# High weights times high and low activations in one 512-column matmul, in five feed-forward phases of a fused three-layer block

## The chip, the cores and the metric

The kernel runs on one core of a Trainium2 chip, as one launch. The metric is the device time in microseconds (us) of that core; the time given for a kernel is the median of its runs. Times of single instructions are given in nanoseconds (ns) where that reads better.

## The reference: what is computed

The input is a sequence of 256 tokens of width 1024, in float32. It goes through three layers, each a mixer and a feed-forward part, with RMS norms before (and in the first layer also after) each part. The mixers (a gated linear recurrence with attention; a gated recurrence in chunks; attention over blocks) are not touched by the change. The feed-forward parts are:

```
# layer 1
h = rms_norm(x, ffn_norm_pre)
up = causal_dwconv(h @ w_up, conv_f_w, conv_f_b)        # 1024 -> 6144, 3 taps
gate, val = split(up)
x = x + rms_norm((gelu(gate) * val) @ w_down, ffn_norm_post)    # 3072 -> 1024
# layers 2 and 3
g, u = split(rms_norm(x, norm_ffn) @ w13)                # 1024 -> 5632
x = x + (silu(g) * u) @ w2                               # 2816 -> 1024
# at the end
return rms_norm(x, final_norm)
```

Every product must come out at close to float32 precision.

## The kernel before

**Layout.** Activations are held transposed: 128 channels on the partitions, 256 tokens along the free axis, one such unit per 128 channels. A weight matrix is cut into *parts* of 128 x 1024 elements, which hold eight 128 x 128 blocks; 374 parts are streamed from memory in the order in which they are used. An output *tile* is 128 output channels by 256 tokens, 256 columns of float32, the lower half of a PSUM bank. Tiles go round four banks (`BANKS`), parts round four slots (`RING`).

**Three products for one.** Each weight and each activation is split in a high and a low half of the type float32r, and a block's product is the sum of three matmuls into the same 256 PSUM columns: high weights by high activations, high weights by low activations, low weights by high activations (`three`, L1337 to L1339). The product of the low halves is left out. Each matmul is issued with a weight load of its own, so the high weights of a block are loaded twice.

**The engines.** Each takes its own list of instructions in order, and semaphores tie the lists together:

- SyncE (SP) starts the transfer of part c into `raw` once part c - 4 has been split.
- ScalarE (ACT) copies `raw` to `w_hi` (`hi`, L270), four parts ahead of TensorE, as soon as TensorE has finished the part whose slot it takes. In the phases `up1` and `up2` it also applies Silu to the gate tiles (L583), and at the head of each loop of four tiles the activation table is loaded (L578).
- VectorE (DVE) makes `w_lo = raw - w_hi` (`lo`, L658), three parts ahead, and takes tiles out of PSUM: in `up1` and `up2` by multiplying them with the norm's factor `RSTD` (`normed`, L694, out of `pair_tile`), in `down1` and `down2` by adding them to the residual `X` (L1117, in `add_branch`).
- GpSimd (POOL) multiplies gate and value and splits the product into `u_hi` and `u_lo` (`products`, L1283 to L1288), and adds up squares for the norms.
- TensorE (PE) waits for a part to be split (`lo_ready`) and for its bank to have been taken out (`evacuated`), then runs the blocks (`tile`, `after_norm`, `down`). `after_norm` runs the first two tiles of a phase block by block as the norm's input is split, then the matmuls that sum the squares (`stat`, L1368), then the rest of the tiles.

**The phases that the change touches**, in the order of the program, with tiles and blocks per tile:

| phase | tiles | blocks per tile | taken out by |
|---|---|---|---|
| `down` (layer 1) | 8 | 24 | ACT, copy to `M` (L500) |
| `up1` (layer 2) | 44 | 8 | DVE, times `RSTD` (L694) |
| `down1` | 8 | 22 | DVE, added to `X` (L1117) |
| `up2` (layer 3) | 44 | 8 | DVE, times `RSTD` (L694) |
| `down2` | 8 | 22 | DVE, added to `X` (L1117) |

After the last tile of `down`, `down1` and `down2` comes a norm. The phase `up` of layer 1, with its three-tap convolution on DVE and ACT, is not touched.

Of the kernel before, what the change touches and what calls it, by code (L numbers as in the profile page):

```python
# [17 lines left out]
ALU = mybir.AluOpType  # L18
# [55 lines left out]
def build(nc, stream, par_d, x_d, wf_d, table_d, onehot_d, ident_d, mask_d, lmask_d, out_d):  # L74
    scr = nc.dram_tensor("bias_rows", [H_MOBA, P, EXT], F32, kind="Internal")
    row = nc.dram_tensor("bias_row", [H_MOBA, EXT], F32, kind="Internal")
    with ExitStack() as ctx:
# [9 lines left out]
        h_hi = sb("h_hi", [P, C, S], F32R)  # L87
        h_lo = sb("h_lo", [P, C, S], F32R)
        u_hi = sb("u_hi", [P, F1, S], F32R)
        u_lo = sb("u_lo", [P, F1, S], F32R)  # L90
# [18 lines left out]

        X = F[:, 52:60, :]  # L110
# [17 lines left out]
        PRA, PRB = F[:, 70:78, :], F[:, 0:8, :]  # L128

# [18 lines left out]
        def dcol(name, e):  # L148
# [51 lines left out]
            sem(n) for n in ("wf_split", "f_normed", "merge_gate_ready", "result_by_pool", "result_scaled"))  # L200
        square_done, b_done, gelu_done = (sem(n) for n in ("decay_squared", "b_done", "gelu_done"))
# [30 lines left out]
        for t in range(R):  # L232
            SCANS.setdefault(H_FOX + 5 + (2 * t + 1) // 3, []).append(t)
        H_COUNT = {n: 8 * i for i, n in enumerate(["mix", "ffn", "n0", "f0", "n1", "f1"])}
# [26 lines left out]
        def _(act):  # L261
# [13 lines left out]
            def out_of(t):  # L275
                return bank[t % BANKS][:, 0:S]

# [217 lines left out]
            for j in range(F1):  # L495
# [70 lines left out]
            def feed(name, per, norm):  # L566

                for j in range(per * C):
                    multiplied(PART[name] + j)
                    if j < per * C - 1:  # L570
                        hi(0, 0, PART[name] + j + HI_AHEAD)
# [54 lines left out]
            for j in range(3 * C):  # L626
                multiplied(PART["down2"] + j)
                hi(0, 0, PART["down2"] + j + HI_AHEAD)
# [19 lines left out]
        def _(dve):  # L648
# [312 lines left out]
            for j in range(F1):  # L961
                step("down", j)
            add_normed("post2", "ffn_post", C, "n0")
# [144 lines left out]
            def add_branch(name, per, norm):  # L1108

                for j in range(per * C):  # L1110
# [4 lines left out]
                    if j % per == per - 1:  # L1115
                        multiplied(PART[name] + j)
# [4 lines left out]
            def swiglu(name, norm, pairs0):  # L1121
# [701 lines left out]
```

## Time and profile before

| | |
|---|---|
| median of 3 runs | 1211.69 us (1211.56 to 1214.74) |
| the profiled execution | 1212.74 us |
| its span in the trace | 1210.9 us |
| busy in the span: PE, weight loads (PEld), DVE, ACT, POOL | 1185.9, 1170.4, 861.0, 681.3, 376.3 us |
| mean granted TensorE clock | 0.994 of full |
| transferred | 204.5 MB, 169 GB/s over the span |

The busy time of an engine is the union of its instructions' times. Matmuls are pipelined, their ends are modelled, and the next one starts before the one before has ended; so how fast TensorE goes is read from the distances between starts, not from durations. A granted clock of 1.00 is 2.4 GHz, one of 0.50 is 1.2 GHz. The chain is the sequence of work that ended last, followed back from the last instruction. The profiled execution took 1.84 us more than its span, and 1.05 us more than the median.

### The profile page before, as it was taken

How to read it: one execution, taken by the hardware profiler on the slowest of the kernel's cores; microseconds unless marked ns; L12 is line 12 of the kernel's file. 1: busy time of each engine (PE TensorE's matmuls, PEld its weight loads, DVE VectorE, ACT ScalarE, POOL GpSimd, SP SyncE). 2: the span in 40 equal slices, each digit the busy share in tenths (PEclk: the TensorE clock that was granted, in tenths of full speed). 3: DMA queues.
4: the chain of work that ended last, by engine and by line, in shares of the span. 5: the costliest groups of instructions: out<-in, count | busy, mean ns of one | idle time of the engine just before them, and what ended most of it. 6: DMA issues, size and time to landing. Idle time of an engine off the chain costs nothing.

```text
span 1210.9 us, 26036 instructions
## 1 busy us (share of the span) xinstructions
PE 1185.9 (98%) x9714; PEld 1170.4 (97%) x9714; DVE 861.0 (71%) x1233; ACT 681.3 (56%) x1019; POOL 376.3 (31%) x403
## 2 busy tenths in 40 slices
PE   8999999999999999998999989999999999999996
PEld 8999999999999999998999989999999999999996
DVE  7877887967799998448898595556666767555644
ACT  6597655654467777345754555555445546555442
POOL 3345000701445555112000165445220006444321
PEclk9999999999999999999999999999999999999999
DMA  6556433476545566653633246556765436555661
GB/s 221 181 190 212 140 105 107 136 264 197 168 140 175 186 188 186 201 175 100 180 104 116 77 158 193 187 176 193 257 194 189 141 122 189 181 185 176 202 199 68
DMA packets 56567, 204.52 MB, mean 169 GB/s; under 512 B 6640, under 2 KB 6776, under 8 KB 56368
## 3 DMA queue, kind: packets, MB, share of 16 engines
q1 hardware_dynamic: 54288, 197.35, 52.5%
q0 software_dynamic: 1632, 5.11, 1.2%
q8 instruction: 52, 0.85, 0.3%
q10 hardware_dynamic: 576, 1.05, 0.2%
q14 instruction: 19, 0.16, 0.0%
HBM read 202.43 MB, written 2.63 MB: 169 GB/s over the span
## 4 chain that ended last, share of the span: by engine, by line
PE 91%; DVE 6%; ACT 1%; DMA 1%; issue 0%; DVEq 0%; SPq 0%; ACTq 0%
PE bank L1337 26%; PE bank L1338 26%; PE bank L1339 26%; PE bank L1596 2%; PE bank L1430 2%; PE bank L1431 2%; PE bank L1432 2%; DVE w_lo L658 1%; PE bank L1519 1%; DVE h_lo L688 1%; DVE work L813 1%; DVE work L712 1%; PE bank L1508 1%; DVE work L679 1%; PE bank L1527 1%; DMA raw<-in_stream 1%
## 5 line engine op out<-in xcount | busy, mean ns | idle before, releaser
L658 DVE TENSOR_TENSOR w_lo<-raw,w_hi 128x1024 fp32r<-128x1024 f32 x374 | 487.6, 1311 | 148.8 <-ACT w_hi L270 145.6
L1337 PE MATMUL bank<-h_hi,w_hi 128*128 128x256 f32 x1888 | 541.9, 287 | 11.2 <-DVE h_lo L688 6.4
L1338 PE MATMUL bank<-h_lo,w_hi 128*128 128x256 f32 x1888 | 535.5, 284 | 0.0
L1339 PE MATMUL bank<-h_hi,w_lo 128*128 128x256 f32 x1888 | 535.4, 284 | 0.0
L270 ACT ACTIVATE w_hi<-raw 128x1024 fp32r<-128x1024 f32 x374 | 392.0, 1053 | 197.8 <-PE bank L1339 187.1
L1337 PEld LDWEIGHTS bank<-h_hi,w_hi 128*128 128x128 f32 x1888 | 363.3, 192 | 17.7 <-issue 7.6
L1338 PEld LDWEIGHTS bank<-h_lo,w_hi 128*128 128x128 f32 x1888 | 363.4, 192 | 0.3
L1339 PEld LDWEIGHTS bank<-h_hi,w_lo 128*128 128x128 f32 x1888 | 363.5, 193 | 0.0
L1337 PE MATMUL bank<-u_hi,w_hi 128*128 128x256 f32 x868 | 247.4, 285 | 3.1 <-DVE u_lo L1082 2.0
L1339 PE MATMUL bank<-u_hi,w_lo 128*128 128x256 f32 x868 | 246.1, 283 | 0.0
L1338 PE MATMUL bank<-u_lo,w_hi 128*128 128x256 f32 x868 | 246.0, 283 | 0.0
L694 DVE TENSOR_TENSOR work<-bank,work 128x256 f32<-128x256 f32 x218 | 90.3, 420 | 123.1 <-PE bank L1339 119.2
L1337 PEld LDWEIGHTS bank<-u_hi,w_hi 128*128 128x128 f32 x868 | 167.1, 192 | 3.9 <-issue 3.4
L1338 PEld LDWEIGHTS bank<-u_lo,w_hi 128*128 128x128 f32 x868 | 167.1, 192 | 0.0
L1339 PEld LDWEIGHTS bank<-u_hi,w_lo 128*128 128x128 f32 x868 | 167.0, 192 | 0.0
L1283 POOL TENSOR_TENSOR work<-work 128x256 f32<-128x256 f32 x68 | 82.6, 1215 | 178.0 <-ACT work L583 119.3
L1288 POOL TENSOR_TENSOR u_lo<-work,u_hi 128x256 f32 x68 | 70.1, 1030 | 11.4 <-POOL u_hi L1286 11.4
L1266 POOL TENSOR_TENSOR work<-work 128x256 f32<-128x256 f32 x39 | 29.8, 765 | 134.7 <-DVE work L1117 79.6
L583 ACT ACTIVATE work<-work 128x256 f32<-128x256 f32 x44 | 18.3, 416 | 74.0 <-PE bank L1339 74.0
L1430 PE MATMUL bank<-w_hi,h_hi 128*128 128x256 f32 x192 | 54.9, 286 | 0.0
L1432 PE MATMUL bank<-w_lo,h_hi 128*128 128x256 f32 x192 | 54.3, 283 | 0.0
L1431 PE MATMUL bank<-w_hi,h_lo 128*128 128x256 f32 x192 | 54.3, 283 | 0.0
(229 smaller groups left out, 1211.2 us busy)
## 6 DMA issues: line engine op xcount, KB each, us to landing
raw<-in_stream SPq DMA_DIRECT2D x374, 512.0 KB, 3.7
bias_rows<-bias_row POOLq DMA_DIRECT2D x1, 1536.0 KB, 15.1
work<-in_x_t SPq DMA_DIRECT2D x2, 512.0 KB, 6.3
work<-in_x_t POOLq DMA_DIRECT2D x1, 1024.0 KB, 6.0
work<-bias_rows POOLq DMA_DIRECT2D x1, 1024.0 KB, 12.6
out<-work ACTq DMA_DIRECT2D x4, 256.0 KB, 2.5
work<-in_lmask POOLq DMA_DIRECT2D x1, 512.0 KB, 7.2
work<-bias_rows POOLq DMA_DIRECT2D x1, 512.0 KB, 8.1
```

The costliest lines, as they stand in the source:

```text
L270: A(w_hi[:, slot, :], raw[:, slot, :], ACT.Copy).then_inc(hi_ready, 1)
L658: v.tensor_tensor(w_lo[:, slot, :], raw[:, slot, :], w_hi[:, slot, :].bitcast(F32), ALU.subtract).then_inc(lo_ready, 1)
L694: v.tensor_tensor(dst, out_of(t), RSTD, ALU.mult).then_inc(evacuated, 1)
L1266: chain.wait(g.tensor_tensor(SQT, src[:, c, :], src[:, c, :], ALU.mult))
L1283: g.tensor_tensor(PB[:, pair, :], GB[:, pair, :], YB[:, 2 * pair + 1, :], ALU.mult).then_inc(pair_free, 1)
L1288: g.tensor_tensor(dst_l, PB[:, pair:pair + 1, :], dst_h.bitcast(F32), ALU.subtract).then_inc(ul_ready, 1)
L1337: mm(out, w_hi[:, slot, s], r_hi, start=start, stop=False)
L1338: mm(out, w_hi[:, slot, s], r_lo, start=False, stop=False)
L1339: return mm(out, w_lo[:, slot, s], r_hi, start=False, stop=stop)
L1430: mm(out, h_hi[:, b, ts], w_hi[:, s0:s0 + 2, f], start=(b == 0), stop=False)
L1431: mm(out, h_lo[:, b, ts], w_hi[:, s0:s0 + 2, f], start=False, stop=False)
L1432: last = mm(out, h_hi[:, b, ts], w_lo[:, s0:s0 + 2, f], start=False, stop=(b == BLK - 1))
```

## The change

The high and low halves of the activations, two tensors before, lie side by side in one (`h_two`, `u_two`), so that a block's high and low activations are 512 columns in a row. In the five phases of the table, `three` is called with `wide`: one matmul of the high weights with all 512 columns, which fills a whole bank (the lower half is high by high, the upper half high by low), and one of the low weights with the 256 high columns, added into the lower half. In the last block of a tile the order of the two is turned round. A block has two matmuls and two weight loads instead of three and three; the number of columns multiplied is the same, 768.

The two halves of a bank then have to be added. ACT copies the upper half to `LOW` in SBUF (`low_half`, 256 columns, after each wide tile), and DVE adds. In `up1` and `up2` the factor `RSTD` takes an instruction of its own. The last tiles of `down`, `down1` and `down2` are done by three matmuls as before.

```diff
-            def three(out, slot, b, r_hi, r_lo, start, stop):
+            def three(t, slot, b, r_two, start, stop, wide=False):
 
                 s = slice(b * P, (b + 1) * P)
-                mm(out, w_hi[:, slot, s], r_hi, start=start, stop=False)
-                mm(out, w_hi[:, slot, s], r_lo, start=False, stop=False)
-                return mm(out, w_lo[:, slot, s], r_hi, start=False, stop=stop)
+                if wide:
+                    pair, own = bank[t % BANKS][:, :], bank[t % BANKS][:, 0:S]
+                    both = r_two.rearrange("p z t -> p (z t)")
+                    if not stop:
+                        mm(pair, w_hi[:, slot, s], both, start=start, stop=False)
+                    last = mm(own, w_lo[:, slot, s], r_two[:, 0, :], start=False, stop=False)
+                    if stop:
+                        last = mm(pair, w_hi[:, slot, s], both, start=False, stop=True)
+                    return last
...
+            def low_half(t):
+                A(LOW[:, t % BANKS, :], bank[t % BANKS][:, S:2 * S], ACT.Copy).then_inc(low_out, 1)
...
@@ ACT, down
-                if j % 3 == 2:
+                    act.wait_ge(evacuated, TILE["down"] + j // 3)
                     A(M[:, j // 3, :], out_of(TILE["down"] + j // 3), ACT.Copy).then_inc(evacuated, 1)
+                elif j % 3 == 2:
+                    low_half(TILE["down"] + j // 3)
...
@@ ACT, up1 and up2
                     for j in range(4):
                         multiplied(PART[name] + j, i, 4)
+                        low_half(TILE[name] + j)
...
@@ DVE, down
+                if j % 3 == 2 and t < C - 1:
+                    dve.wait_ge(low_out, LOW_BEFORE["down"] + t + 1)
+                    v.tensor_tensor(M[:, t, :], out_of(TILE["down"] + t), LOW[:, (TILE["down"] + t) % BANKS, :],
+                                    ALU.add).then_inc(evacuated, 1)
...
@@ DVE, down1 and down2
-                        multiplied(PART[name] + j)
+                        if per == 3 and t < C - 1:
+                            dve.wait_ge(low_out, LOW_BEFORE[name] + t + 1)
+                            low = LOW[:, (TILE[name] + t) % BANKS, :]
+                            chain.wait(v.tensor_tensor(X[:, t, :], X[:, t, :], low, ALU.add))
+                        else:
+                            multiplied(PART[name] + j)
                         v.tensor_tensor(X[:, t, :], X[:, t, :], out_of(TILE[name] + t), ALU.add).then_inc(evacuated, 1)
...
@@ DVE, up1 and up2
-                    multiplied(PART[name] + j, i, 4)
                     if j % 2 == 0:
                         dve.wait_ge(pair_free, lin(i, 2, pairs0 + j // 2 + 1))
-                    normed(YB[:, j, :] if j % 2 else GR[:, j // 2, :], TILE[name] + j)
+                    dst = YB[:, j, :] if j % 2 else GR[:, j // 2, :]
+                    dve.wait_ge(low_out, lin(i, 4, LOW_BEFORE[name] + j + 1))
+                    v.tensor_tensor(dst, out_of(TILE[name] + j), LOW[:, (TILE[name] + j) % BANKS, :],
+                                    ALU.add).then_inc(half_added, 1)
                     if not first:
                         lo(i, 4, PART[name] + j + LO_AHEAD)
+                    dve.wait_ge(half_added, lin(i, 4, HALVES[name] + j + 1))
+                    v.tensor_tensor(dst, dst, RSTD, ALU.mult).then_inc(evacuated, 1)
```

How the matmuls of a tile stand on PE at the start of `down` (each row is a matmul with the weight load ahead of it), before:

```order
L1337 MATMUL bank<-u_hi,w_hi 128x256
L1338 MATMUL bank<-u_lo,w_hi 128x256
L1339 MATMUL bank<-u_hi,w_lo 128x256
L1337 MATMUL bank<-u_hi,w_hi 128x256
L1338 MATMUL bank<-u_lo,w_hi 128x256
L1339 MATMUL bank<-u_hi,w_lo 128x256
```

and with the change:

```order
L1372 MATMUL bank<-u_two,w_hi 128x512
L1373 MATMUL bank<-u_two,w_lo 128x256
L1372 MATMUL bank<-u_two,w_hi 128x512
L1373 MATMUL bank<-u_two,w_lo 128x256
L1372 MATMUL bank<-u_two,w_hi 128x512
L1373 MATMUL bank<-u_two,w_lo 128x256
```

Two blocks take six instructions before, four with the change, of which every second is 512 columns wide.

How the instructions stand on DVE at the start of `up1` (`w_lo` is the split of a part, `work<-bank` takes a tile out of PSUM), before:

```order
L679 RECIPROCAL work<-work 128x256 [waits rms_ready]
L694 TENSOR_TENSOR work<-bank,work 128x256 [waits pair_free,part_done,rstd_ready]
L694 TENSOR_TENSOR work<-bank,work 128x256 [waits part_done]
L658 TENSOR_TENSOR w_lo<-raw,w_hi 128x1024 [waits hi_ready]
L694 TENSOR_TENSOR work<-bank,work 128x256 [waits pair_free,part_done]
L658 TENSOR_TENSOR w_lo<-raw,w_hi 128x1024 [waits hi_ready]
L694 TENSOR_TENSOR work<-bank,work 128x256 [waits part_done]
L658 TENSOR_TENSOR w_lo<-raw,w_hi 128x1024 [waits hi_ready]
```

and with the change:

```order
L696 RECIPROCAL work<-work 128x256 [waits rms_ready]
L1157 TENSOR_TENSOR work<-bank,work 128x256 [waits low_half_out,pair_free,rstd_ready]
L1162 TENSOR_TENSOR work<-work 128x256 [waits half_added]
L1157 TENSOR_TENSOR work<-bank,work 128x256 [waits low_half_out]
L675 TENSOR_TENSOR w_lo<-raw,w_hi 128x1024 [waits hi_ready]
L1162 TENSOR_TENSOR work<-work 128x256 [waits half_added]
L1157 TENSOR_TENSOR work<-bank,work 128x256 [waits low_half_out,pair_free]
L675 TENSOR_TENSOR w_lo<-raw,w_hi 128x1024 [waits hi_ready]
L1162 TENSOR_TENSOR work<-work 128x256 [waits half_added]
L1157 TENSOR_TENSOR work<-bank,work 128x256 [waits low_half_out]
L675 TENSOR_TENSOR w_lo<-raw,w_hi 128x1024 [waits hi_ready]
L1162 TENSOR_TENSOR work<-work 128x256 [waits half_added]
```

Each tile has two instructions around the split instead of one ahead of it; the first waits for ACT's copy of the upper half (`low_half_out`), and the second, behind the split, is the one that sets the bank free. On ACT, in the loop of `up1` (two tiles of four; `w_hi` is the high copy of a part, `work<-work` the Silu), before:

```order
L269 ISA [waits part_done]
L270 ACTIVATE w_hi<-raw 128x1024 [waits part_landed2]
L273 REGISTER_ALU
L582 REGISTER_ALU [waits part_done]
L583 ACTIVATE work<-work 128x256 [waits evacuated]
L270 ACTIVATE w_hi<-raw 128x1024 [waits part_landed3]
```

and with the change:

```order
L280 ISA
L286 ACTIVATE work<-bank 128x256 [waits part_done]
L276 ISA
L277 ACTIVATE w_hi<-raw 128x1024 [waits part_landed2]
L280 REGISTER_ALU
L286 ACTIVATE work<-bank 128x256 [waits part_done]
L597 REGISTER_ALU
L598 ACTIVATE work<-work 128x256 [waits evacuated]
L277 ACTIVATE w_hi<-raw 128x1024 [waits part_landed3]
```

A copy out of PSUM stands ahead of each high copy, and ahead of the Silu.

## Rows read from the trace of the kernel before

**Rows 1.** The page, part 1 and the clock row of part 2 (40 slices).

```profile
PE 1185.9 (98%) x9714; PEld 1170.4 (97%) x9714; DVE 861.0 (71%) x1233; ACT 681.3 (56%) x1019; POOL 376.3 (31%) x403
...
PEclk9999999999999999999999999999999999999999
```

**Rows 2.** The page, part 4: the chain that ended last, shares by engine.

```profile
PE 91%; DVE 6%; ACT 1%; DMA 1%; issue 0%; DVEq 0%; SPq 0%; ACTq 0%
```

**Rows 3.** Windows inside down, up1, down1 and down2 (up2 reads as up1).

```profile
core 0: us, PE busy (x) PEld busy (x) DVE busy (x) ACT busy (x) POOL busy (x), PEclk, DMA share, GB/s
471.80:540.00 68.20, 68.20 (x569) 68.02 (x568) 37.03 (x30) 29.98 (x36) 14.92 (x18) 1.00 0.63 195
719.00:838.00 119.00, 119.00 (x994) 119.00 (x994) 70.11 (x87) 68.35 (x87) 56.84 (x63) 1.00 0.59 183
842.00:902.00 60.00, 60.00 (x502) 60.00 (x501) 36.58 (x37) 26.92 (x30) 16.83 (x18) 1.00 0.74 229
...
1139.00:1200.00 61.00, 61.00 (x510) 61.00 (x510) 28.46 (x28) 25.57 (x29) 15.18 (x16) 1.00 0.52 157
```

**Rows 4.** Timeline of PE inside up1: start us, us, engine, line; 42 intervals between these.

```profile
739.80 0.28 PE L1338 MATMUL bank<-h_lo,w_hi 128*128 128x256 f32 x1
...
744.84 0.28 PE L1338 MATMUL bank<-h_lo,w_hi 128*128 128x256 f32 x1
```

**Rows 5.** PE timeline and window at a half-clock stretch; 8 intervals between the two.

```profile
330.14 0.41 PE L1339 MATMUL bank<-h_hi,w_lo 128*128 128x256 f32 x1
...
331.84 0.41 PE L1338 MATMUL bank<-h_lo,w_hi 128*128 128x256 f32 x1
...
330.00:331.80 1.80, 1.80 (x10) 1.80 (x10) 1.80 (x6) 1.55 (x4) 0.65 (x1) 0.50 0.00 0
```

**Rows 6.** PE timeline, forget-gate matmuls with 16-column weights; 23 intervals between the two.

```profile
43.81 0.28 PE L1467 MATMUL bank<-h_hi,u_hi 128*16 128x256 f32 x1
...
46.42 0.28 PE L1469 MATMUL bank<-h_hi,u_lo 128*16 128x256 f32 x1
```

**Rows 7.** The chain in order of time: start, us, what.

```profile
337.31 1.29 PE bank L1387 x6
```

**Rows 8.** Groups of instructions, weight loads (PEld): busy us, mean ns.

```profile
L1337 PEld LDWEIGHTS bank<-h_hi,w_hi 128*128 128x128 f32 x1888 | 363.3, 192 | 17.7 <-issue 7.6 <-DVE w_lo L658 5.6 <-DVE h_lo L688 4.0
...
L1467 PEld LDWEIGHTS bank<-h_hi,u_hi 128*16 128x16 f32 x8 | 0.8, 94 | 0.1
```

**Rows 9.** Groups of instructions on ACT and DVE: busy us, mean ns, idle before.

```profile
L270 ACT ACTIVATE w_hi<-raw 128x1024 fp32r<-128x1024 f32 x374 | 392.0, 1053 | 197.8 <-PE bank L1339 187.1 <-DMA raw<-in_stream 8.7 <-issue 1.6
...
L578 ACT ACT_TABLE_LOAD x22 | 28.2, 1283 | 0.4
...
L583 ACT ACTIVATE work<-work 128x256 f32<-128x256 f32 x44 | 18.3, 416 | 74.0 <-PE bank L1339 74.0
...
L500 ACT ACTIVATE work<-bank 128x256 f32<-128x256 f32 x8 | 3.1, 383 | 11.4 <-PE bank L1339 11.4
...
L658 DVE TENSOR_TENSOR w_lo<-raw,w_hi 128x1024 fp32r<-128x1024 f32 x374 | 487.6, 1311 | 148.8 <-ACT w_hi L270 145.6 <-ACT work L431 3.0
L694 DVE TENSOR_TENSOR work<-bank,work 128x256 f32<-128x256 f32 x218 | 90.3, 420 | 123.1 <-PE bank L1339 119.2 <-POOL work L1283 2.8
...
L703 DVE TENSOR_TENSOR work<-work 128x256 f32<-128x256 f32 x8 | 4.4, 549 | 0.1
```

**Rows 10.** Timelines of PE, ACT and DVE at the start of up1.

```profile
718.62 0.47 PE L1337 MATMUL bank<-h_hi,w_hi 128*128 128x256 f32 x1
...
719.01 0.47 ACT L281 ACTIVATE work<-bank,derived 128x256 f32<-128x256 f32 x1 [1.28 <-PE bank L1368]
...
713.67 1.63 DVE L658 TENSOR_TENSOR w_lo<-raw,w_hi 128x1024 fp32r<-128x1024 f32 x1
...
719.52 1.75 DVE L679 RECIPROCAL work<-work 128x256 f32<-128x256 f32 x1 [0.51 <-ACT work L281]
...
721.98 1.23 DVE L658 TENSOR_TENSOR w_lo<-raw,w_hi 128x1024 fp32r<-128x1024 f32 x1
```

More of the change, by code:

```diff
@@ L233, in build @@
             SCANS.setdefault(H_FOX + 5 + (2 * t + 1) // 3, []).append(t)
+        LOW_BEFORE, _n = {}, 0
+        for name, n_tiles in (("down", C - 1), ("up1", 2 * F2), ("down1", C - 1), ("up2", 2 * F2), ("down2", C - 1)):
+            LOW_BEFORE[name] = _n
+            _n += n_tiles
+        HALVES = {"up1": 0, "up2": 2 * F2}
         H_COUNT = {n: 8 * i for i, n in enumerate(["mix", "ffn", "n0", "f0", "n1", "f1"])}
@@ L569, in feed @@
                     multiplied(PART[name] + j)
+                    if per == 3 and j % 3 == 2 and j // 3 < C - 1:
+                        low_half(TILE[name] + j // 3)
                     if j < per * C - 1:
@@ L627, in _ @@
                 multiplied(PART["down2"] + j)
+                if j % 3 == 2 and j // 3 < C - 1:
+                    low_half(TILE["down2"] + j // 3)
                 hi(0, 0, PART["down2"] + j + HI_AHEAD)
@@ L1344, in free_bank, with tile @@
                     pe.wait_ge(evacuated, lin(i, m, t - BANKS + 1))
-            def tile(i, c, t, x_hi=h_hi, x_lo=h_lo, low=None, n0=0, blocks=range(BLK)):
+            def tile(i, c, t, x_two=h_two, low=None, n0=0, blocks=range(BLK), wide=False):
                 if blocks[0] == 0:
@@ L1396, in columns, with after_norm @@
                 last.then_inc(col_mm, 1)
-            def after_norm(norm, name, n):
+            def after_norm(norm, name, n, wide=False):
                 c, t = PART[name], TILE[name]
@@ L1405, in after_norm @@
                     for j in range(2):
-                        last = three(bank[(t + j) % BANKS][:, 0:S], (c + j) % RING, b, h_hi[:, b, :], h_lo[:, b, :],
-                                     b == 0, b == BLK - 1)
+                        last = three(t + j, (c + j) % RING, b, h_two[:, b, :, :], b == 0, b == BLK - 1, wide)
                         if b == BLK - 1:
@@ L1414, in after_norm @@
                 for j in (2, 3):
-                    tile(0, c + j, t + j)
-                tiles(c + 4, t + 4, n - 4)
+                    tile(0, c + j, t + j, wide=wide)
+                tiles(c + 4, t + 4, n - 4, wide=wide)
             def token_tile(c, t, n, tok, low=None, n0=0):
@@ L1485, in _ @@
                     for k, f in enumerate(GATE_IN[o]):
-                        last = three(out, c % RING, b, u_hi[:, 5 * g + f, :], u_lo[:, 5 * g + f, :], k == 0,
+                        last = three(out, c % RING, b, u_two[:, 5 * g + f, :, :], k == 0,
                                      k == len(GATE_IN[o]) - 1)
@@ L1661, in _ @@
             for t in range(3, C):
-                tile(0, PART["ho"] + t, TILE["ho"] + t, u_hi, u_lo)
-            after_norm("f0", "up1", 2 * F2)
+                tile(0, PART["ho"] + t, TILE["ho"] + t, u_two)
+            after_norm("f0", "up1", 2 * F2, wide=True)
             down("down1", F2, F1)
@@ L1694, in first @@
             def first(t, blocks):
-                tile(0, PART["mo"] + t, TILE["mo"] + t, u_hi, u_lo, y_lo, C, blocks)
+                tile(0, PART["mo"] + t, TILE["mo"] + t, u_two, y_lo, C, blocks)
             first(0, range(0, 6))
@@ L1707, in _ @@
             for t in range(3, C):
-                tile(0, PART["mo"] + t, TILE["mo"] + t, u_hi, u_lo)
-            after_norm("f1", "up2", 2 * F2)
+                tile(0, PART["mo"] + t, TILE["mo"] + t, u_two)
+            after_norm("f1", "up2", 2 * F2, wide=True)
             down("down2", F2, F1 + F2)
```

32 lines of the change are left out of this document (18 added, 14 removed).

## The prediction

> **What bounds the kernel now.** I read the page's busy times first: PE is busy for 1185.9 us of 1210.9, the loads for 1170.4, at full clock in almost every slice [rows 1]. Matmul busy time alone can hide waits, so next the chain that ended last: 91% of it is PE [rows 2]. Then the windows inside the five phases: PE has no idle time in any, while DVE is busy for 59% of `up1` (70.11 of 119.00), ACT for 57%, POOL for 48%, and the transfers take 0.52 to 0.74 of the DMA engines [rows 3]. So the time of these phases is the number of matmuls times the distance between their starts. That distance is in the timeline: 42 intervals between 739.80 and 744.84 us, 120.0 ns each, at granted clock 1.00 [rows 3, 4]. A block is three of them, 360 ns.
>
> How much of the 120 ns is columns? In the one stretch with matmuls of this form at granted clock 0.50 (1.2 GHz), eight intervals take 1.70 us, 213 ns each [rows 5]. That is 256 columns at one per cycle and nothing else; at 2.4 GHz the columns are then 106.7 ns, and 13.3 ns of each 120 are something else. The change leaves the columns alone (768 per block) and can win only from this rest.
>
> **What the rest is.** Three groups bear on it. With weights of 16 columns instead of 128 the same moving operand comes every 2.61 us / 23 = 113.5 ns [rows 6], and such a load is recorded with 94 ns, not 192 [rows 8]. So the size of the load decides at least 6.5 of the 13.3 ns. At half clock, where a matmul lasts 213 ns, a full load adds nothing [rows 5]: it is done beside the matmul before it. And the matmuls that sum squares (plain float32, 128 weight columns, recorded as two passes each) take six passes in 1.29 us, 215 ns each [rows 7], close to the length that a 512-column matmul must have (512 / 2.4 = 213.3). I conclude that at full clock a 256-column matmul ends before the next load is ready, and 120 ns is the time of a load; a matmul of 213 ns covers its successor's load.
>
> **The change part by part.**
>
> *The matmuls.* Wide blocks: `down` 7 tiles x 24 = 168, `up1` 44 x 8 = 352, `down1` 7 x 22 = 154, `up2` 352, `down2` 154, together 1180. A block becomes one wide matmul and one narrow. The wide one is bounded below by 213.3 ns, and above by two narrow ones, 240. I take 215, the summing row, which is nearest in length and weights [rows 7]. The narrow one I leave at 120, since the load for the next block still has only it for cover; its lower bound is 113.5 [rows 6]. Block: 335 ns for 360, so 25 ns x 1180 = 29.5 us.
>
> The Trainium skill ("TensorE: Matmul & The Clock Gate", section "Part 3: Packing small matmuls — row/col tiling") says that a weight load overlaps running matmuls only where the row group differs, which is not so here. The same page's section on fast weight load has a load in 32 cycles in theory, and 256 + 32 cycles at 2.4 GHz are exactly 120.0 ns; by that rule the estimate for the sum would be 13.3 ns per load taken away, 15.7 us and not 29.5. The half-clock row speaks against it.
>
> *The copies on ACT.* One per wide tile, 383 ns by the copy in `down` [rows 9]. In `up1` ACT then has per tile 1.05 (high copy) + 0.38 + half a Silu 0.21 + a quarter of a table load 0.32 = 1.96 us, beside a PE tile of 8 x 335 = 2.68 us. Hidden; so in the down phases, where ACT was busy for under half.
>
> *The adds on DVE.* In `up1` 0.42 for the add out of PSUM, 1.31 for the split, and the multiplication by `RSTD`, an SBUF-only operation which has 0.549 in the row of the same kind [rows 9]: 2.28 us of 2.68. Hidden. In the down phases 0.42 to 0.55 more per three parts, beside an idle half.
>
> *Waits that are new.* DVE now waits for ACT's copy, and ACT's Silu for DVE's multiplication, which stands behind the split. Over four tiles that closes a ring: two Silus 0.84, two high copies 2.10, a table load 1.28, two low copies 0.76, two adds 0.84, two splits 2.62, two multiplications 1.10, together 9.54 us. The handover that the timeline shows is 0.04 us (square root ended 719.48, reciprocal began 719.52 [rows 10]); ten of them make 9.94. PE needs 4 x 2.68 = 10.72. The ring fits, with 7% to spare; a bank is set free later than before, but three tiles ahead of need.
>
> *The start of `up1` and `up2`.* Here DVE and ACT catch up after the norm. Before: reciprocal ends at 721.27, the split for tile 4 at 721.98 + 1.23 = 723.21 [rows 10]. After: ACT 719.48 + table 1.28 + copy 0.38 + high copy 1.05 + copy 0.38 = 722.57, DVE add 0.42, split 1.3: 724.3. PE starts tile 2 at 718.62 [rows 10] and is through tiles 2 and 3 after 5.36 us, at 724.0. A stall of 0.3 us, twice: 0.6 us. Bounds 0 and 1.5.
>
> *The rest.* The last tiles and with them the norms' entry keep their form; the extra `evacuated` wait of ACT in `down` is for a tile that ended a whole tile earlier. `up` is untouched. The transfers must come faster, in `down1` 229 x 360/335 = 246 GB/s at 0.74 x 360/335 = 0.80 of the DMA engines [rows 3]; SP issues them as before. Cost 0.
>
> Sum: 29.5 - 0.6 = 28.9 us. The profiled execution took 1212.74 us, 1.84 more than its span, so it would take 1183.8; it lies 1.05 over the median, and against the median of 1211.69 I forecast **1182.8 us**.
>
> **The rivals**, with the time at the median:
>
> - *A fixed cost per full-rate matmul* of 113.5 - 106.7 = 6.8 ns stays [rows 6]: the wide one takes 220.1, the block 340.1, gain 23.5 - 0.6: 1188.8. For: the only row of the same type with a small load. Against: no such rest at half clock [rows 5].
> - *The load is serial*, or the rest grows with the columns (6.8 ns per 256 gives 226.9 for the wide one as 213.3 + 13.3 gives 226.6): block 347, gain 15.5 - 0.3: about 1196.5. For: 288 cycles to the digit. Against: rows 5, 6.
> - *The narrow one gets shorter too*, 113.5, if the load runs ahead by more than one matmul: block 328.5, gain 37.2 - 0.8: 1175.3. Against: in `up1` 994 equal matmuls take 119.0 us [rows 3], so nothing shows such a reserve.
> - *No gain*: a 512-column matmul takes 240: 1212.
> - *Slower: the ring in `up1` and `up2` becomes the bound.* With the split at the longest that the timeline shows, 1.63 [rows 10], the multiplication twice its row because POOL works in SBUF beside it, and handovers of 0.15, the ring takes 9.54 + 0.64 + 1.10 + 1.50 = 12.8 us, 3.20 per tile instead of 2.88: 88 x 0.32 = 28 us lost, 476 x 0.025 = 11.9 us won in the down phases: about 1228. It costs something from 10.72 us on, and decides the sign from 4 x (2.88 + 11.9/88) = 12.06. Against: 9.94 by the rows. Halfway, the gain is merely smaller.
> - *A wide matmul of 131 ns.* No row here has a matmul of this form spaced closer than its columns; at that price the ring would bind first, at 9.94 / 4 = 2.49 us per tile, and the time would be 88 x 0.39 + 476 x 0.109 = 86 us shorter, about 1126. The Trainium skill (the same page, section "Back-to-back issue gap") gives about 131 ns per matmul of 512 columns in a real stream with loads, and 216 for one alone. The trace bears out the second kind of figure only: it has 215.
>
> **How the numbers follow.** Forecast 0.44, fixed cost 0.23, serial load 0.16, shorter narrow 0.07, ring 0.06 (half of it a smaller gain, half slower), no gain 0.03, 131 ns 0.01. Faster by over 0.3% (about what a measurement of this kernel can tell from no change): 0.94; within: 0.03; slower: 0.03. The range takes in the forecast with its bounds (wide at 213.3 and no stall: 1180; 2 us for the runs' scatter below that), the fixed cost and the serial load: 1178 to 1197. Left out are about 0.16.
>
> **What would show it.** In the timeline of PE inside `up1`, starts 215 and 120 ns apart in turn (right), 220 and 120 (fixed cost), 227 and 120 (serial). The window of `up1` shorter by 44 x 0.2 = 8.8 us with PE busy throughout; a wait of PE on `w_lo` only at tile 4. If PE shows idle time before every fourth tile with ACT or DVE as the releaser, the ring binds. I am wrong if the distances are right and the sum isn't, or if DVE or ACT is busy for over 0.95 of `up1`.

## The result, and the profile after

The changed kernel takes 1204.3 us (median of 4 runs, 1202.72 to 1204.74), the kernel before, run beside it, 1212.96 (4 runs, 1211.56 to 1214.74). The ratio is 0.9928, with an interval of 0.9915 to 0.994: faster by 8.7 us, in direction as forecast and in size less than a third of the 28.9 us; 1204.3 lies above the range of 1178 to 1197. The kernel before came out 1.3 us above the 1211.69 from which the forecast was counted, so the gains are what is compared.

The profiled execution took 1202.72 us, span 1200.9, so 10.0 less than the one before; some 1.5 of them are a stretch at half clock outside the changed phases that the one before had and this one had not (experiment 3). Its page, busy times and chain:

```profile
PE 1176.5 (98%) x8534; PEld 1107.2 (92%) x8534; DVE 910.9 (76%) x1342; ACT 708.8 (59%) x1121; POOL 388.4 (32%) x403
...
PE 90%; DVE 6%; ACT 1%; DMA 1%; issue 1%; POOL 0%; DVEq 0%; SPq 0%; POOLq 0%; ACTq 0%
```

Against [rows 1, 2] PE is still the bound, with nearly the same share of the chain (90% for 91%). So the time is still the number of matmuls times their distance. The windows of four of the five phases, with the columns of [rows 3]:

```profile
core 0: us, PE busy (x) PEld busy (x) DVE busy (x) ACT busy (x) POOL busy (x), PEclk, DMA share, GB/s
471.80:539.00 67.20, 67.07 (x404) 59.34 (x403) 37.82 (x38) 30.31 (x37) 20.58 (x19) 1.00 0.64 201
719.00:838.00 119.00, 119.00 (x678) 103.53 (x677) 94.04 (x132) 78.80 (x130) 58.60 (x64) 1.00 0.59 188
842.00:902.00 60.00, 60.00 (x376) 53.77 (x375) 40.93 (x47) 31.12 (x40) 18.62 (x17) 1.00 0.71 232
1139.00:1190.00 51.00, 51.00 (x312) 45.30 (x311) 25.90 (x29) 24.06 (x31) 13.31 (x13) 1.00 0.48 148
```

In `up1` (the second window) PE is busy throughout, at full clock. DVE is busy for 94.04 us of 119 (0.79), up from 70.11 [rows 3]; ACT for 0.66. The same 119 us held 994 matmuls before, 331 blocks of three; now 678, which are 339 blocks of two. That is 2.3% more work in the time, where 360 to 335 ns would have been 7%.

The timeline of PE there, one row per matmul (start, recorded length, engine and line):

```profile
739.62 0.40 PE L1372 MATMUL bank<-h_two,w_hi 128*128 128x512 f32 x1
739.85 0.28 PE L1373 MATMUL bank<-h_two,w_lo 128*128 128x256 f32 x1
739.97 0.40 PE L1372 MATMUL bank<-h_two,w_hi 128*128 128x512 f32 x1
740.21 0.28 PE L1373 MATMUL bank<-h_two,w_lo 128*128 128x256 f32 x1
740.33 0.40 PE L1372 MATMUL bank<-h_two,w_hi 128*128 128x512 f32 x1
...
741.03 0.40 PE L1372 MATMUL bank<-h_two,w_hi 128*128 128x512 f32 x1
```

Only the distances between starts count; the recorded lengths overlap. From 739.62 to 741.03 four blocks pass: 1.41 us, 352.5 ns each. A wide matmul holds the engine for 230 to 240 ns, a narrow one for 110 to 120. Over 964 such pairs of this trace at full clock the means are 234.8 and 116.9, together 351.7 ns; over whole tiles of `up1`, whose last block has the other order, a block takes 352.4. I reckon with 352.1, between the two: 7.9 ns less than 360, times 1180, is 9.3 us. The result is 8.7 with an interval of some 7 to 10 us.

The waits inside `up1` show who stands still for whom (waiting for what: us in total, times, longest):

```profile
POOL work L1314 <- DVE work L1162: 56.3, 22, 6.5
ACT work L286 <- PE bank L1375: 34.7, 28, 1.5
DVE work L1157 <- ACT work L286: 24.9, 37, 1.2
```

PE waits for nobody. DVE waits for ACT's copy (L286) and ACT for PE: the feed side has time left over.

### The profile page after: what moved, and what is told of

It reads as the page before. It is cut to its first block, busy times and chain, and to the rows that moved or that the text cites. A ratio compares the mean times of both kernels' runs of the same rounds, so it can differ in the third digit from the quotient of the medians.

```text
span 1200.9 us, 23974 instructions
## 1 busy us (share of the span) xinstructions
PE 1176.5 (98%) x8534; PEld 1107.2 (92%) x8534; DVE 910.9 (76%) x1342; ACT 708.8 (59%) x1121; POOL 388.4 (32%) x403
## 4 chain that ended last, share of the span: by engine, by line
PE 90%; DVE 6%; ACT 1%; DMA 1%; issue 1%; POOL 0%; DVEq 0%; SPq 0%; POOLq 0%; ACTq 0%
PE bank L1372 20%; PE bank L1378 15%; PE bank L1380 14%; PE bank L1379 14%; PE bank L1373 11%; PE bank L1633 2%; PE bank L1375 2%; PE bank L1469 2%; PE bank L1470 2%; PE bank L1471 2%; DVE w_lo L675 2%; PE bank L1557 1%; DVE h_two L705 1%; DVE work L830 1%; DVE work L729 1%; PE bank L1546 1%
## 5 line engine op out<-in xcount | busy, mean ns | idle before, releaser
L1378 PE MATMUL bank<-h_two,w_hi 128*128 128x256 f32 x1184 | 342.7, 289 | 8.0 <-DVE h_two L705 5.3
L1380 PE MATMUL bank<-h_two,w_lo 128*128 128x256 f32 x1184 | 336.8, 284 | 0.0
L1379 PE MATMUL bank<-h_two,w_hi 128*128 128x256 f32 x1184 | 336.8, 284 | 0.0
L1378 PEld LDWEIGHTS bank<-h_two,w_hi 128*128 128x128 f32 x1184 | 228.9, 193 | 14.1 <-issue 7.6
L1379 PEld LDWEIGHTS bank<-h_two,w_hi 128*128 128x128 f32 x1184 | 229.0, 193 | 0.2
L1380 PEld LDWEIGHTS bank<-h_two,w_lo 128*128 128x128 f32 x1184 | 228.9, 193 | 0.0
L1372 PE MATMUL bank<-h_two,w_hi 128*128 128x512 f32 x616 | 221.3, 398 | 2.5 <-DVE w_lo L675 2.5
L1373 PE MATMUL bank<-h_two,w_lo 128*128 128x256 f32 x704 | 183.6, 281 | 0.0
L1372 PE MATMUL bank<-u_two,w_hi 128*128 128x512 f32 x455 | 160.9, 397 | 0.0
L1372 PEld LDWEIGHTS bank<-h_two,w_hi 128*128 128x128 f32 x616 | 115.9, 188 | 26.9 <-DVE w_lo L675 2.7
L1373 PEld LDWEIGHTS bank<-h_two,w_lo 128*128 128x128 f32 x704 | 132.9, 189 | 7.9
L1373 PE MATMUL bank<-u_two,w_lo 128*128 128x256 f32 x476 | 130.4, 281 | 0.1
L1378 PE MATMUL bank<-u_two,w_hi 128*128 128x256 f32 x392 | 112.1, 286 | 3.1 <-DVE u_two L1104 2.0
L1379 PE MATMUL bank<-u_two,w_hi 128*128 128x256 f32 x392 | 110.9, 283 | 0.0
L1380 PE MATMUL bank<-u_two,w_lo 128*128 128x256 f32 x392 | 110.9, 283 | 0.0
L1319 POOL TENSOR_TENSOR u_two<-work,u_two 128x256 f32 x68 | 98.5, 1449 | 12.5 <-POOL u_two L1317 12.5
L286 ACT ACTIVATE work<-bank 128x256 f32<-128x256 f32 x109 | 41.3, 379 | 95.2 <-PE bank L1375 95.2
L1373 PEld LDWEIGHTS bank<-u_two,w_lo 128*128 128x128 f32 x476 | 89.9, 189 | 2.3 <-POOL u_two L1319 0.5
```

The lines of the kernel that those rows point to most:

```text
L286: A(LOW[:, t % BANKS, :], bank[t % BANKS][:, S:2 * S], ACT.Copy).then_inc(low_out, 1)
L1319: g.tensor_tensor(dst_l, PB[:, pair:pair + 1, :], dst_h.bitcast(F32), ALU.subtract).then_inc(ul_ready, 1)
L1372: mm(pair, w_hi[:, slot, s], both, start=start, stop=False)
L1373: last = mm(own, w_lo[:, slot, s], r_two[:, 0, :], start=False, stop=False)
L1378: mm(out, w_hi[:, slot, s], r_two[:, 0, :], start=start, stop=False)
L1379: mm(out, w_hi[:, slot, s], r_two[:, 1, :], start=False, stop=False)
```

## Experiments

Gains are against the kernel before, run on the same chip. The changed kernel itself was run again twice with 5 runs, beside experiments 3 to 5 and beside 6 and 7 (not beside 1 and 2): 1204.8 (ratio 0.9941, 0.9928 to 0.9955) and 1203.69 (0.9925, 0.9912 to 0.9939), against 1211.91 and 1212.75. With the first comparison its gain is 8.7, 7.1 and 9.1 us. Diffs are against the changed kernel.

### 1. Matmul forms alone, on a quiet chip

Behind the last norm's matmuls a tail of further matmuls was put, whose results nobody uses: mostly 24 of a form, with nothing else at work. The diff shows two of 16 series.

```diff
+            for k in range(24):
+                mm(B5[:, :], wt(2 * k), act2(k), start=(k == 0), stop=False)
+                mm(B5[:, 0:S], wt(2 * k + 1), act2(k)[:, 0:S], start=False, stop=(k == 23))
+            for k in range(24):
+                mm(B5[:, :], wt(k), act2(k), start=(k == 0), stop=(k == 23))
...
```

> The changed kernel with a tail of matmuls after the last norm, when the other engines are quiet: 24 each of several forms, so that the distance between starts can be read per form (columns moved x columns of weights). Theory A (a load beside the running matmul is free unless the matmul is shorter than the load): 512x128 comes every 215 ns, 512x16 as well, 384x128 every 162, 128x128 and 64x128 both every 120 (the load). Theory B (each load with its matmul costs a fixed 13.3 ns that nothing hides): 512x128 226.7, 384x128 173.3, 256x128 120, 128x128 66.7. Theory C (B, and the wide matmul also loses time to the other engines' use of memory in the phases): here 226.7, where the phases showed 230 to 241, and wide and narrow in turn 346.7 per block. If wide and narrow in turn stay at 352 here as in the phases, the other engines have no part in it.

First, wide matmuls in a row (L1759), 16 weight columns in place of 128 (L1765), and 384 columns (L1773):

```profile
1213.73 0.39 PE L1759 MATMUL bank<-u_two,w_hi 128*128 128x512 f32 x1
...
1216.90 0.39 PE L1759 MATMUL bank<-u_two,w_hi 128*128 128x512 f32 x1
...
1228.00 0.39 PE L1765 MATMUL bank<-u_two,w_hi 128*16 128x512 f32 x1
...
1229.85 0.40 PE L1765 MATMUL bank<-u_two,w_hi 128*16 128x512 f32 x1
...
1243.79 0.33 PE L1773 MATMUL bank<-u_two,w_hi 128*128 128x384 f32 x1
...
1245.69 0.33 PE L1773 MATMUL bank<-u_two,w_lo 128*128 128x384 f32 x1
```

14 intervals in 3.17 us are 226.4 ns; over the whole settled series it is 226.7. The 384 columns take 11 intervals in 1.90 us, 173 ns. With the 120.0 of 256 columns the three lie on one line: columns / 2.4 plus 13.3 ns. Using the same weights over and over, or two banks in turn, changes nothing (226.7 in both). Eight intervals of the 16-column form take 1.85 us, 231 ns: the small load makes a long matmul no shorter, though it makes the short one shorter (256 columns by 16 weight columns: 116.7; by 64: 113.3).

Of the expectations, B and C had 512, 384 and 256 columns right. At 128 columns all missed, A with 120 ns and B with 66.7:

```profile
1247.19 0.28 PE L1775 MATMUL bank<-u_two,w_lo 128*128 128x128 f32 x1
...
1249.42 0.28 PE L1775 MATMUL bank<-u_two,w_lo 128*128 128x128 f32 x1
```

20 intervals in 2.23 us are 112 ns, and 64 columns (L1777) take as long. So with weights of 128 columns there is a floor of about 112 ns that a matmul of 256 columns, at 120, is already above. Whether the floor is the time of a load was not tested.

Next the clock. Behind the series of 128 and 64 columns, in which PE had work without a pause, the next one (L1779) began at half clock, and its window shows it (columns as above):

```profile
1252.83 0.63 PE L1779 MATMUL bank<-u_two,w_lo 128*128 128x512 f32 x1
...
1254.96 0.63 PE L1779 MATMUL bank<-u_two,w_hi 128*128 128x512 f32 x1
```
```profile
1252.80:1255.00 2.20, 2.20 (x7) 1.69 (x6) 0.00 (x0) 0.00 (x0) 0.00 (x0) 0.50 0.03 7
```

Five intervals in 2.13 us, 426 ns, are 512 / 1.2 = 426.7 and nothing more. At granted clock 0.50 the 13.3 ns are gone for a long matmul as for a short one [rows 5]. The half-clock row therefore told of the clock, and not of a load that a longer matmul hides.

The Trainium skill ("TensorE: Matmul & The Clock Gate", section "Wait — 56ns, not 53.3ns?") says just this of the form: the distance is columns / 1.2 GHz exactly at the low clock, and columns / 2.4 GHz plus a fixed amount at the high one. Its amount is about 2.5 ns; the runs here have 13.3 for this matmul type, and the measurement decides.

Last the mixture, wide and narrow in turn, with all other engines silent:

```profile
1205.63 0.40 PE L1756 MATMUL bank<-u_two,w_hi 128*128 128x512 f32 x1
1205.87 0.28 PE L1757 MATMUL bank<-u_two,w_lo 128*128 128x256 f32 x1
...
1207.75 0.40 PE L1756 MATMUL bank<-u_two,w_hi 128*128 128x512 f32 x1
```
```profile
1204.20:1212.00 7.80, 7.80 (x47) 6.76 (x46) 0.00 (x0) 0.00 (x0) 0.00 (x0) 1.00 0.01 2
```

Six blocks in 2.12 us are 353 ns, where the settled values of the two forms sum to 346.7. So turning from one length to the other costs some 6.7 ns per block, and neither DVE nor a transfer has part in it. Two wide, then two narrow, gave 348.3.

### 2. The feed side kept, the wide matmuls taken back

In a wide tile only the first and the last block are still wide; in the others the product with the low activations goes into the upper half by a matmul of its own. The copies, adds and waits of ACT and DVE stay.

```diff
-                    if not stop:
-                        mm(pair, w_hi[:, slot, s], both, start=start, stop=False)
...
+                        mm(own, w_hi[:, slot, s], r_two[:, 0, :], start=False, stop=False)
+                        mm(low, w_hi[:, slot, s], r_two[:, 1, :], start=False, stop=False)
...
```

> The changed kernel with its copies, adds and waits as they are, but in all blocks of a wide tile except the first and the last the wide matmul is two of 256 columns again, high by high into the lower half of the bank and high by low into the upper. 962 of 1180 blocks are split. If the feeding engines cost nothing and the whole gain is the matmuls' (theory A, B and C alike), those blocks take 360 ns each and the time is the kernel before's less 218 x 7.9 ns = 1.7 us: ratio 0.9986. If the new copies and adds cost time on the path, or writing to two halves of a bank does, it comes out slower than the kernel before.

Measured 1209.68 (11 runs), ratio 0.9979 (0.997 to 0.9988). The window of `up1`:

```profile
719.00:830.00 111.00, 111.00 (x860) 107.52 (x859) 86.76 (x122) 74.69 (x124) 54.03 (x60) 1.00 0.62 186
```

DVE is as busy as in the changed kernel (0.78), and PE still has no gap. The kernel gained 3.1 us by the medians (2.5 by the ratio, 1.5 to 3.6) with 218 wide blocks left, where 218 x 7.9 gives 1.7: if the copies and adds cost PE anything, it is not to be seen. One tile of `up1`, 22 matmuls from last to last:

```profile
725.68 0.40 PE L1377 MATMUL bank<-h_two,w_hi 128*128 128x512 f32 x1
...
728.52 0.40 PE L1377 MATMUL bank<-h_two,w_hi 128*128 128x512 f32 x1
```

That is 2.84 us for 2.88 before, with only two wide blocks, and over the five phases of the trace 3.6 us. A wide block here saves some 17 ns, twice the 7.9. Here the two stand side by side, and all other matmuls are narrow: the saving is not the same in every order. The lost gain is not on the feed side; the theory that work on ACT or DVE slows the matmuls falls, here for the narrow ones, and in experiment 1 for the mixture, which is as slow without them.

### 3. Only the down phases wide

`up1` and `up2` are as before the change; `down`, `down1` and `down2` keep 476 wide blocks.

```diff
-            after_norm("f0", "up1", 2 * F2, wide=True)
+            after_norm("f0", "up1", 2 * F2)
...
-            after_norm("f1", "up2", 2 * F2, wide=True)
+            after_norm("f1", "up2", 2 * F2)
```

> The wide form in down, down1 and down2 alone, up1 and up2 as in the kernel before. If the gain is a sum over blocks, it is 476 x (360 - 351.4) ns = 4.1 us, ratio 0.9966, and up1 and up2 the other 5.8 us. If the copies and adds of up1 and up2 cost time on the path, the share of the down phases is larger than that.

Measured 1209.95 (11 runs), ratio 0.9979 (0.997 to 0.9988): a gain of 2.5 us by the ratio (1.5 to 3.6), where 476 x 7.9 is 3.8 and the expected 0.9966 lies just outside the interval. The traces show where the rest is. From the start of the first matmul to that of the last, `down`, `down1` and `down2` take 69.23, 63.24 and 63.24 us before the change, and 68.20, 62.05 and 62.05 here: 3.4 us less, 7.2 ns per block. In the changed kernel they take 67.82, 62.05 and 62.05, and `up1` and `up2`, from the third tile on, 118.3 each for 121.0, which is 8.0 ns per block. So both kinds of phase gain by their blocks, 9.1 us in all; a saving per block asks for that, and a bound in one kind of phase does not.

In the profiled execution the missing part lies outside the changed phases, in the mixer ahead of `up1`. The same stretch of the program (598.29 to 718.62 us before) took 121.82 us in this profiled execution and 120.33 in that of the kernel before. The first row is of this run, the second of the kernel before:

```profile
713.20:716.40 3.20, 3.20 (x18) 3.20 (x17) 2.92 (x5) 0.88 (x2) 2.61 (x4) 0.50 0.60 196
713.00:716.40 3.40, 3.40 (x31) 3.40 (x30) 3.37 (x6) 0.64 (x2) 2.46 (x4) 1.00 0.49 154
```

Here PE went at half clock, after 4.00 us in which it was busy for 1.55; both had such a stretch near 680 us as well. Over nine traces this part of the program takes 118.7 to 118.8 us with no stretch at half clock (the changed kernel's profiled execution among them), 120.2 to 120.3 with one, 121.8 with two: about 1.5 us each. That may be a good part of the scatter between runs.

### 4. Equal lengths together, in all wide tiles

If each turn costs, matmuls of one length should stand together: per part first a wide one (it has to open the bank), then all narrow ones, then the other wide ones.

```diff
+            def grouped(t, slot, x_two, k0, n, start, stop, ready=None):
...
+                for b in ahead:
+                    if ready is not None:
+                        pe.wait_ge(ul_ready, ready + k0 + b + 1)
+                    last = high(b, start and b == 0, False)
+                if ready is not None:
+                    pe.wait_ge(ul_ready, ready + k0 + n)
+                for b in range(n):
+                    last = low(b)
+                for b in range(n):
+                    if b not in ahead:
+                        last = high(b, False, stop and b == n - 1)
+                return last
```

> The changed kernel with the matmuls of a part put in another order: in a tile of up1 and up2 the first wide one, then all eight narrow ones, then the other seven wide ones; in the down phases likewise by part. Nothing else is changed. Theory B (every float32r matmul at full clock costs its columns and 13.3 ns, and turning between wide and narrow costs some 6.7 ns per block more): a block comes to 346.7 ns and a part pays the settling of some 27 ns once, as in the wide-only run of the first tail: 350.0 instead of 352.1, 2.4 us faster than the changed kernel, ratio to the kernel before about 0.990. If the further 5.4 ns per block come from the other engines or from where the operands lie, the order changes nothing. Theory A (a load hides only under a long matmul) expects it slower in the narrow group and no better in the wide one.

Measured 1205.06 (5 runs), ratio 0.995 (0.9937 to 0.9964), against 0.9941 for the changed kernel beside it: no gain in the time. In `up1` and `up2` the order did bring what was expected of it, 349.2 ns per block over whole tiles for 352.4. The timeline of PE at the start of `down` says where that went (in brackets the idle time before a row, and what ended it), with the window behind it:

```profile
474.87 2.00 PE L1385 MATMUL bank<-u_two,w_hi 128*128 128x512 f32 x8
479.61 1.27 PE L1387 MATMUL bank<-u_two,w_lo 128*128 128x256 f32 x8 [2.74 <-POOL u_two L1319]
480.68 1.91 PE L1385 MATMUL bank<-u_two,w_hi 128*128 128x512 f32 x4
```
```profile
480.50:484.00 3.50, 3.50 (x11) 2.83 (x10) 1.19 (x2) 0.00 (x0) 0.00 (x0) 0.51 0.56 181
```

In the first tile of a down phase the products `u_two` arrive from POOL one by one. The group of narrow matmuls of the tile's third part (the second row) waits until all eight products of that part are there, while block by block PE does seven of the eight blocks ahead of the last product. So PE stood still for 2.74 us, and then went on at half clock for some 3 us, where a wide matmul takes 427 ns.

### 5. More mixtures, and plain float32

Another tail of unused matmuls: other groupings, 512 and 384 columns in turn, and the type of the summing matmuls, whose 215 ns [rows 7] had been taken for the wide one.

```diff
+            for k in range(16):
+                mm(B5[:, 0:S], ident[:, :], X[:, k % C, :], start=True, stop=True)
...
+            for k in range(12):
+                mm(B5[:, :], ident[:, :], F[:, 52 + k % 4:54 + k % 4, :], start=True, stop=True)
```

> The changed kernel with a second tail. Blocks as wide, narrow, narrow, wide; four wide then four narrow; eight and eight; wide, narrow, narrow; 512 and 384 in turn; and plain float32 with 256 and 128 columns. Theory B: the sum of columns / 2.4 + 13.3 ns per matmul is a floor for all float32r forms (a block 346.7), and what is above it counts the turns between lengths: least in eight and eight, between 346.7 and 350. Plain float32 keeps about 2 ns of rest per pass of 256 columns (215 ns) and 112 ns with 128 columns, which would show that the 13.3 ns belong to float32r at full rate, not to loads as such.

The plain float32 series, each row one group of passes (two recorded per matmul):

```profile
1249.74 4.91 PE L1778 MATMUL bank<-work,ident 128*128 128x256 f32 x22
1254.49 3.73 PE L1780 MATMUL bank<-work,ident 128*128 128x128 f32 x32
1258.06 10.47 PE L1782 MATMUL bank<-work,ident 128*128 128x512 f32 x24
```

From start to start 22 passes of 256 columns take 4.75 us, 216 ns, and 32 of 128 columns 3.57 us, 112 ns, the floor of experiment 1 again. The granted clock was 1.00. So a pass of 256 columns of plain float32 runs at half the rate and carries 2.5 ns (215.8 over the whole series) over 213.3; 512 take 429. The 215 ns of [rows 7] were right as a number and belonged to another instruction. As for grouping, wide-narrow-narrow-wide and eight wide then eight narrow both gave about 349 ns per block, so longer groups bring no more than pairs; 512 and 384 in turn gave about 413, against 400 by the settled values.

### 6. Grouped, but the first tile of a down phase block by block

```diff
-                    for b in range(min(BLK, KT - BLK * (j % 3))):
-                        k = BLK * (j % 3) + b
-                        if j < 3:
-                            pe.wait_ge(ul_ready, n0 + k + 1)
-                        last = three(t, c % RING, b, u_two[:, k, :, :], k == 0, k == KT - 1, j // 3 < C - 1)
+                    n = min(BLK, KT - BLK * (j % 3))
+                    if 0 < j // 3 < C - 1:
+                        last = grouped(t, c % RING, u_two, BLK * (j % 3), n, j % 3 == 0, j % 3 == 2)
+                    else:
...
```

> The grouped order of the run before it, but in the first tile of each down phase block by block as in the changed kernel, since there the grouped order waited for products that POOL had not yet made (a pause of 3.1 us at 476 us and one of 1.3 us at 842 us in its trace, with a stretch of half clock behind the first). Theory B: without those the order shows its 349 ns per block for 352 and the kernel is 2.5 to 3.5 us faster than the changed one, ratio about 0.990 to 0.991. If the order truly brings nothing, it stands where the changed kernel stands.

Measured 1200.91 (4 runs), ratio 0.9907 (0.9891 to 0.9922): 2.8 us faster than the changed kernel beside it, and the fastest version of this study. The intervals overlap, but its four runs (1200.48 to 1201.78) all lie below the five of the changed kernel (1202.62 to 1204.86), and in the traces of the two the five phases differ by 3.4 us. PE in `up1`:

```profile
739.89 1.12 PE L1387 MATMUL bank<-h_two,w_lo 128*128 128x256 f32 x8
740.84 2.00 PE L1385 MATMUL bank<-h_two,w_hi 128*128 128x512 f32 x8
742.68 0.52 PE L1387 MATMUL bank<-h_two,w_lo 128*128 128x256 f32 x3
```

The eight wide ones are seven of this tile and the first of the next; from narrow to narrow a tile takes 2.79 us, where eight blocks of 352.1 are 2.82.

### 7. The last tiles wide as well

The change leaves out the last tile of a phase that leads to a norm. Here those of `down1` and `down2` are wide too.

```diff
-                if j % 3 == 2 and j // 3 < C - 1:
+                if j % 3 == 2:
                     low_half(TILE["down2"] + j // 3)
...
-                        if per == 3 and t < C - 1:
+                        if per == 3:
```

> The changed kernel with the last tiles of down1 and down2 wide as well. By the rows: 22 blocks x 7.9 ns = 0.17 us less on PE for each, and behind the last matmul ACT's copy (0.38), the add of the low half (0.42) and two handovers more on the way to the norm, some 0.9 us. Slower than the changed kernel by about 0.7 us at each of two places, 1.4 us in all, ratio about 0.995; in the trace the first statistics matmul of the norm starts that much later behind the last block.

Measured 1205.11 (5 runs), ratio 0.9934 (0.9921 to 0.9948): 1.4 us slower than the changed kernel beside it. The intervals of the two overlap, so the time alone leaves it at "not faster"; the timelines ahead of the last norm, the last matmul of `down2` and then DVE, show the mechanism. First the changed kernel in this comparison, then this one:

```profile
1191.39 0.28 PE L1380 MATMUL bank<-u_two,w_lo 128*128 128x256 f32 x1
...
1191.71 0.42 DVE L1144 TENSOR_TENSOR work<-work,bank 128x256 f32<-128x256 f32 x1 [6.60 <-PE bank L1380]
1193.96 1.75 DVE L696 RECIPROCAL work<-work 128x256 f32<-128x256 f32 x1 [1.83 <-ACT work L291]
```
```profile
1191.65 0.40 PE L1375 MATMUL bank<-u_two,w_hi 128*128 128x512 f32 x1
...
1192.58 0.42 DVE L1141 TENSOR_TENSOR work<-work 128x256 f32<-128x256 f32 x1 [6.97 <-ACT work L286]
1193.04 0.42 DVE L1144 TENSOR_TENSOR work<-work,bank 128x256 f32<-128x256 f32 x1
1195.21 1.75 DVE L696 RECIPROCAL work<-work 128x256 f32<-128x256 f32 x1 [1.75 <-ACT work L291]
```

The last add (L1144) used to follow PE at once. Now ACT's copy (L286, 0.38) and another add (L1141, 0.42) stand between, with nothing on PE to cover them, and the add starts 1.39 us behind the last matmul's start for 0.32 before: 1.07 us more, where 22 wide blocks save 0.2. At the norm behind `down1` the add comes 0.9 us later in the same way, but PE has other matmuls meanwhile, and the reciprocal of that norm starts only 0.5 us later (903.10 for 902.62). Less the blocks' saving the two come to about the 1.3 us by which the spans differ; expected was 0.7 at each.

## Why the prediction was wrong in size

**What bounds the kernel.** Right. PE had no gap in the phases after the change either, and 1180 blocks times a change in distance gives the measured gain.

**The rest of 13.3 ns per matmul.** Right, and the columns are as worked out (106.7 and 213.3 ns).

**"A matmul of 213 ns covers its successor's load."** This is the step that failed. The 13.3 ns are not the part of a load that sticks out of a short matmul: at full clock every matmul of this type has them, at 256, 384 and 512 columns alike (experiment 1). What may be a load that sticks out shows only at 128 and 64 columns, as a floor of 112 ns, and the 120 ns of 256 columns lie above it. So merging two saves about the rest of one, and the wide matmul is 226.7 ns where I put 215. All three supports of the step gave way:
- [rows 5] has no rest at half clock. I read that as cover by a longer matmul. But 512 columns at half clock, 427 ns, have no rest either, and 512 at full clock, as long as 256 at half, have all of it. It goes with the clock, not with the length.
- [rows 7] is plain float32 at half rate, with a rest of its own of 2.5 ns (experiment 5). Nearest in length and weights, it was farthest in what counted, the type and with it the rate.
- [rows 6], smaller weights and 113.5 ns, is true of short matmuls only: at 512 columns the smaller load bought nothing (231 ns), and at 256 in experiment 1 only 3.3 ns of the 6.5.

**The mixture.** No term stood for it. The two lengths in turn cost 352.1 per block against 346.7 for the sum of their settled distances.

In numbers: 335 forecast, 352.1 measured, 17.1 x 1180 = 20.2 us more; 11.7 ns of it (13.8 us) are the rest of the wide matmul, 5.4 (6.3 us) the alternation.

**The rivals.** *Serial load, or a rest that grows with the columns* had the size of the wide matmul right, 226.6 for 226.7, and the block at 347; with the alternation its 1196.5 becomes about 1203. Its first name is not thereby shown, since same weights and smaller weights did not shorten a 512-column matmul, and its second is wrong, since the rest does not grow: 13.3 ns at 256, 384 and 512. *Fixed cost* had the right mechanism, a constant per matmul at full clock that is not there at half, with the wrong constant: 6.8 ns, from the one form with a small load (experiment 1 has 116.7 ns for it, not 113.5). *Ring*: no sign. DVE is at 0.79 of `up1`, PE never waits, and the multiplication L1162 takes 0.41 to 0.97 us. *131 ns* and *no gain* are out by the same rows.

**Copies, adds and transfers at no cost.** Right (experiment 2). Had the block been 335 ns, the ring would have had less room; that was not tried.

**The stall at the start of `up1`.** Forecast 0.3 us twice, measured none. DVE and PE (the first matmul of tile 2, and of tile 4) in the changed kernel:

```profile
716.24 0.58 PE L1372 MATMUL bank<-h_two,w_hi 128*128 128x512 f32 x1
...
717.14 1.75 DVE L696 RECIPROCAL work<-work 128x256 f32<-128x256 f32 x1 [0.41 <-ACT work L291]
...
720.49 1.21 DVE L675 TENSOR_TENSOR w_lo<-raw,w_hi 128x1024 fp32r<-128x1024 f32 x1
...
722.04 0.40 PE L1372 MATMUL bank<-h_two,w_hi 128*128 128x512 f32 x1
```

The split for tile 4 ended at 721.70, 2.81 us after the reciprocal, where I had reckoned with 3.0. PE's tile 4 began at 722.04 and its tile 2 at 716.24, where the second matmul came 0.2 us later than elsewhere. With tiles of 2.68 us PE would, by this estimate, have come to tile 4 at about 721.8, 0.1 us behind the split. So the lead was sized slightly too pessimistically, but it is too close to say that there would have been no stall; the slower blocks made the lead larger.

**The last tile left out.** The prediction took it as free; experiment 7 prices the other choice at about 1.4 us.

**What stays open.** What the 13.3 ns are. A load always belongs to a matmul of this type, so none could be timed without one. The Trainium skill ("TensorE: Matmul & The Clock Gate", section "Weight-path perf modes — Fast Weight Load (FWL) and DoubleRow") has a load in 32 cycles in theory, which it gives for 8-bit floats, and 32 cycles at 2.4 GHz are an estimate of 13.3 ns; the sum by that rule in the prediction, 15.7 us less, was nearer than mine. The trace agrees in the number only and cannot say that it is the load. Against a load that always comes on top speak the half-clock rows, where nothing is over. Open too is why two lengths in turn cost more than each alone, and what the floor of 112 ns is.

## What to carry to other kernels

Merging matmuls that share weights saves about the fixed rest of each one removed (here 13.3 ns of 120), less where the lengths then alternate (7.9); price a new size from rows of the same type at the same clock, and take no half-clock row for a proof that something is hidden. Where lengths mix, put equal ones together, except where the operands still arrive one by one. An extra copy out of PSUM is free behind a matmul stream and costs its whole length, with the add behind it, where PE has nothing else to do ahead of a norm (1.07 us at the last one).

## What the runs showed of the hardware that I had not expected

- At full clock a float32r matmul costs columns / 2.4 + 13.3 ns (120.0, 173, 226.7 at 256, 384, 512), whatever the bank and with the same or changing weights; at half clock 427 ns at 512, with nothing on top. Below 256 columns it stops falling: 128 and 64 columns with 128 weight columns both take 112 ns, and so does a pass of 128 columns of plain float32.
- Alternating 512 and 256 columns costs about 6.7 ns per pair beyond the sum, also into two banks, with every other engine silent; two of each in turn still 1.6, eight of each 2.7. After a change to wide the first six distances were 233, 236, 228, 233, 230 and 227 ns before it settled.
- Sixteen weight columns make a 512-column matmul slower, 231 ns for 226.7, and a 256-column one faster, 116.7 for 120.0.
- A pause of 2.74 us on PE was followed by about 3 us at granted clock 0.51. In that trace (experiment 4) the matmuls of `down` take 71.6 us, without the pause (experiment 6) 67.6: the wait cost some 4 us, about one and a half times its length.
- A stretch of about 3 us at half clock in the mixer ahead of `up1` costs 1.5 us, and whether there is none, one or two of them changes from execution to execution (experiment 3).
